# Token norms and router sums of a fused two-block transformer layer laid in four strips of 128 tokens

## The reference, cut to what matters

```python
def rms_norm(x, g):                       # five of these, over the 1024 channels of a token
    r = lax.rsqrt(jnp.mean(x * x, axis=-1, keepdims=True) + EPS)
    return x * r * g
# block 1
h = rms_norm(x, norm1_g); p = h @ w_in    # 1024 x 3328
...                                       # gMLP branch, S5 branch, gates, w_up_a, w_up_b, w_out
h2 = rms_norm(x, norm2_g)
probs = softmax(h2 @ w_router)            # 16 experts
gate, idx = lax.top_k(probs.T, 64)        # 64 tokens for each expert
...                                       # for each expert: silu(xs @ w_gate) * (xs @ w_up) @ w_down
x = rms_norm(x + scattered, final_g)
# block 2
u = rms_norm_2(x, norm1_gain); proj = u @ w_in_2
y_lru = rms_norm_2(scan(...) * gelu(g_lru), lru_norm_gain)    # over 512 channels
o = head_group_norm(retention(q, k, v), ret_norm_gain)        # 4 heads of 128 channels
x = x + concat(y_lru, o * silu(g_ret)) @ w_out_2
up = conv(rms_norm_2(x, norm2_gain) @ ffn_up_w)               # 1024 x 6144, two halves
x = x + (gelu(up_a) * up_v) @ ffn_down_w
return rms_norm_2(x, final_norm_gain)
```

## Time and profile before

| | |
|---|---|
| median of 3 runs | 1932.91 us (1932.58 to 1933.05) |
| profiled execution, its own time | 1933.91 us |
| span in its trace, first to last instruction | 1932.1 us |
| PE busy | 1750.1 us, 91% |
| DVE busy | 667.9 us, 35% |
| ACT busy | 443.6 us, 23% |
| DMA moved | 492.47 MB |
| mean granted clock of PE | 0.982 |

### The profile page before, as it was taken

How to read it: one execution, slowest core, us unless ns; L and a number is a source line. 1 busy time by engine, 2 the same in 40 slices (tenths; PEclk the granted TensorE clock), 3 DMA queues, 4 the chain that set the end, 5 groups by cost and what they waited for, 6 DMA issues and landing times. The chain is left out here.

```text
span 1932.1 us, 19429 instructions
## 1 busy us (share of the span) xinstructions
PE 1750.1 (91%) x8120; PEld 1045.2 (54%) x8120; DVE 667.9 (35%) x903; ACT 443.6 (23%) x546; POOL 0.2 (0%) x4
## 2 busy tenths in 40 slices
PE   5998997899998898988979889789999999999997
PEld 4877774434342332423324233247767778888885
DVE  6865463201011010100101001047735466555644
ACT  4433322101010000100001010055433343323332
POOL 0000000000000000000000000000000000000000
PEclk9999999899999999999999999999999999999999
DMA  4313644699999999999999999950412213232311
GB/s 160 99 48 107 218 136 184 261 428 428 427 428 429 429 428 429 428 429 428 428 428 429 428 428 428 428 220 28 153 44 88 87 66 109 87 109 87 109 44 44
DMA packets 76389, 492.47 MB, mean 255 GB/s; under 512 B 7472, under 2 KB 12592, under 8 KB 51504
## 3 DMA queue, kind: packets, MB, share of 16 engines
q1 hardware_dynamic: 76336, 491.71, 63.1%
HBM read 487.49 MB, written 2.10 MB: 253 GB/s over the span
## 5 line engine op out<-in xcount | busy, mean ns | idle before, releaser
L1166 PE MATMUL ps<-xs,xe 128*64 128x512 f32 x2048 | 462.9, 600 | 65.8 <-DMA xs<-w_up 33.2
L1166 PEld LDWEIGHTS ps<-xs,xe 128*64 128x64 f32 x2048 | 142.1, 137 | 379.2 <-issue 265.9
L1178 PE MATMUL ps<-xs,hidT 128*64 128x512 f32 x1024 | 229.7, 596 | 13.6 <-DMA xs<-w_down 8.9
L412 DVE TENSOR_TENSOR lo<-raw,hi 128x2048 fp32r<-128x2048 f32 (+1 forms) x73 | 164.9, 2259 | 217.7 <-ACT hi L403 210.6
L1394 DVE TENSOR_TENSOR hid<-hid,ps 128x512 f32<-128x512 f32 x32 | 20.6, 684 | 524.3 <-PE ps L1166 524.3
L403 ACT ACTIVATE hi<-raw 128x2048 fp32r<-128x2048 f32 (+1 forms) x73 | 137.9, 1889 | 232.0 <-PE ps L466 96.9
L466 PE MATMUL ps<-xh,hi 128*128 128x512 f32 x416 | 167.8, 403 | 10.3 <-DVE ga L921 5.8
L466 PE MATMUL ps<-xl,hi 128*128 128x512 f32 x416 | 164.3, 395 | 0.0
L442 PE MATMUL ps<-xh,hi 128*128 128x512 f32 x384 | 151.4, 394 | 4.3 <-ACT hi L403 3.2
L1178 PEld LDWEIGHTS ps<-xs,hidT 128*64 128x64 f32 x1024 | 74.0, 137 | 147.6 <-issue 127.7
L442 PE MATMUL ps<-xl,hi 128*128 128x512 f32 x384 | 150.2, 391 | 0.0
(11 more groups left out here) (415 smaller groups left out, 1783.6 us busy)
## 6 DMA issues: line engine op xcount, KB each, us to landing
xs<-w_up SPq DMA_DIRECT2D x64, 2048.0 KB, 32.8
xs<-w_gate SPq DMA_DIRECT2D x64, 2048.0 KB, 31.9
xs<-w_down SPq DMA_DIRECT2D x64, 2048.0 KB, 31.3
raw<-w_in SPq DMA_DIRECT2D x25, 1024.0 KB, 7.2
raw<-ffn_up_w SPq DMA_DIRECT2D x24, 1024.0 KB, 5.1
raw<-ffn_down_w SPq DMA_DIRECT2D x12, 1024.0 KB, 5.1
raw<-w_out SPq DMA_DIRECT2D x8, 1024.0 KB, 5.1
xin<-x_t SPq DMA_DIRECT2D x4, 512.0 KB, 7.4
```

The lines of the kernel that those rows point to most:

```text
L412: dve.tensor_tensor(lo[slot][:, 0:size], raw[:, raw_slot(n), 0:size], hi[slot][:, 0:size].bitcast(F32), ALU.subtract).then_inc(sem("lo_don ...
L1166: mm = pe.matmul(ps[64 * half:64 * half + 64, bank + b, :], xe[:, k, CAP * u:CAP * (u + 1)], xs[n % NXS][:, f:f + 512], start=(k == 0), st ...
L1178: mm = pe.matmul(ps[64 * nn:64 * nn + 64, YB, :], hidT[:, 4 * (c % 2) + kk, CAP * half:CAP * (half + 1)], xs[n % NXS][:, kk * D + nn * 512 ...
```

## The change

Sums go into four strips of 32 partitions, one for each 128 tokens, all in the same 128 columns of a bank. A strip's 32 rows are equal, so root and reciprocal need 128 columns in place of 512. Then four matmuls with a 32-row operand that has a one in its first row spread each strip back over all partitions, each into a bank of its own, and ACT copies the 512 values to SBUF.

```diff
@@ new helpers
+        def strip_sums(pe, i, bank):
+            for k in range(KD):
+                pe.wait_ge(sem("nrm_sq"), NSQ[i] + k + 1)
+                for t in range(NT):
+                    mm = pe.matmul(strip(bank, t), ones[:, 0:32], squares(i)[0][:, k, t * P:(t + 1) * P],
+                                   start=(k == 0), stop=(k == KD - 1))
+            mm.then_inc(sem("nrm_ps"), 1)
+        def strip(bank, t, c=0):
+            return ps[32 * t:32 * t + 32, bank, c:c + P]
+        def strip_spread(pe, r, bank, c):
+            for t in range(NT):
+                mm = pe.matmul(ps[:, bank + t, c:c + P], pick[32 * t:32 * t + 32], r[32 * t:32 * t + 32],
+                               start=True, stop=True)
+            return mm
+        def strip_root(act, i, bank):
...
+            act.activation(rs[0], ps[:, bank, 0:P], ACT.Sqrt, scale=1.0 / D, bias=eps).then_inc(sem("nrm_rms"), 1)
@@ norm 1, PE
-            norm_sums(pe, 0, QQ + 3)
+            strip_sums(pe, 0, QQ + 3)
+            def spread_first():
+                pe.wait_ge(sem("rb_done"), 1)
+                strip_spread(pe, rs[0], PP, SW)
+                pe.transpose(ps[:, PP, SW + P:SW + 2 * P], rs[0], ident).then_inc(sem("rt_ps"), 1)
             chunk_mms(pe, 1, QQ, 0, 4, xh, xl, True, closes=False,
-                      after={(0, 2): lambda: pe.wait_ge(sem("nrm_rms"), 1)})
-            pe.wait_ge(sem("rb_done"), 1)
-            for t in range(NT):
-                mm = pe.matmul(ps[:, PP, SW + t:SW + t + 1], rb[:, t * P:(t + 1) * P], ident[:, 0:1], start=True, stop=True)
+                      after={(0, 1): spread_first, (0, 2): lambda: pe.wait_ge(sem("nrm_rms"), 1)})
@@ router, PE
-                mm = pe.matmul(ps[o, LB, :], wrg[:, k, :], xt[:, k, :], start=(k < 4), stop=(k >= 4))
...
+                for t in range(NT):
+                    pe.matmul(strip(LB, t), wrg[:, k, :], xt[:, k, t * P:(t + 1) * P], start=(k == 0), stop=False)
+                pe.wait_ge(sem("nrm_sq"), KD + k + 1)
+                for t in range(NT):
+                    mm = pe.matmul(strip(LB, t), hot[:, 0:32], sqx[:, k, t * P:(t + 1) * P], start=False, stop=(k == KD - 1))
...
+            for bank in (SB, LB):
+                mm = pe.transpose(ps[:, bank, 0:P], part[:], ident)
@@ router, ACT
-            a(part[1][:], ps[:, SB, :], ACT.Copy).then_inc(sem("part_done"), 1)
@@ first norm of block 2, PE: after two tiles of chunk N2+1
+            def spread_two():
+                pe.wait_ge(sem("rms_step"), 1)
+                for q in range(4):
+                    pe.matmul(ps[:, QQ + q, 256:512], pick[32 * q:32 * q + 32], rr[32 * q:32 * q + 32], start=True, stop=True)
+                for b in range(2):
+                    mm = pe.transpose(ps[:, QQ + 1, b * P:(b + 1) * P], rr[:, b * P:(b + 1) * P], ident)
+                mm.then_inc(sem("rt_ps"), 1)
@@ LRU and heads, PE
-                    mm = pe.matmul(ps[:, 0, :], ones, xc[:, m, :], start=(m == 0), stop=(m == 3))
+                    for t in range(NT):
+                        mm = pe.matmul(strip(0, t), ones[:, 0:32], xc[:, m, t * P:(t + 1) * P], start=(m == 0), stop=(m == 3))
...
+                      after={(0, 0): head_vars, (0, 1): spread_lru, (0, 3): spread_heads})
-            pe.wait_ge(sem("mix_lo"), 4)
             pe.wait_ge(sem("yn_done"), RH)
-            chunk_mms(pe, N2 + 12, PP, 0, 4, mh, ml, closes=False)
+            chunk_mms(pe, N2 + 12, PP, 0, 4, mh, ml, closes=False, by_tile=("mix_lo", 1))
@@ FFN norm, PE
-            norm_sums(pe, 4, QQ + 3)
-            chunk_mms(pe, NFFN + 1, QQ, 0, 4, xh, xl, closes=False,
-                      after={(0, 2): lambda: pe.wait_ge(sem("nrm_rms"), 4)})
-            chunk_mms(pe, NFFN + 2, PP, 4, 4, xh, xl, opens=False, by_tile=("xl_done", 2 * KD + 5))
-            chunk_mms(pe, NFFN + 3, QQ, 4, 4, xh, xl, opens=False)
+            strip_sums(pe, 4, QQ + 3)
...
+            chunk_mms(pe, NFFN + 1, PP, 4, 4, xh, xl, opens=False, by_tile=("xl_done", 2 * KD + 5), after={1: spread_fourth})
+            pe.wait_ge(sem("spr_out"), 3)
+            for h in range(2):
+                chunk_mms(pe, NFFN + 2 + h, QQ, 4 * h, 4, xh, xl, opens=(h == 0), closes=(h == 1))
```

More of the change, by code:

```diff
@@ L265, in build @@
         sqx = at("sqx", [P, KD, SEQ], F32, B + 57)
-        part = [at(f"part{j}", [P, SEQ], F32, B + 51 + 2 * j) for j in range(2)]
+        part = at("part", [P, P], F32, B + 51)
         cst2 = at("cst2", [P, NCONST - NSMALL], F32, B + 38)
@@ L328, in build @@
         vmean = sm[:, 32:48]
+        hot = sm[:, 150:198]
         pick = sm[:, 256:384]
+        rs = [sm[:, 384 + 128 * j:512 + 128 * j] for j in range(2)]
         def lz(j):
@@ L477, in chunk_mms @@
                             mm = one(part, m, kk)
+                    if kk in after:
+                        after[kk]()
             elif each:
@@ L837, in first_dve @@
             dve.memset(eps, EPS).then_inc(sem("eps_done"), 1)
+            dve.memset(pick, 0.0)
+            L(dve.memset(hot, 0.0))
+            for h in range(4):
+                dve.memset(pick[32 * h:32 * h + 1], 1.0)
+            dve.memset(hot[:, 16:17], 1.0)
             dve.wait_ge(sem("cst_in"), 32)
@@ L1492, in head_vars, with spread_lru, spread_heads @@
                     pe.wait_ge(sem("csq_done"), h + 1)
-                    mm = pe.matmul(ps[32 * h:32 * h + 32, 1, :], ones[:, 0:32], kr[:, h, :], start=True, stop=True)
+                    for t in range(NT):
+                        mm = pe.matmul(strip(1, t, P), hot[:, 16 - h:48 - h], kr[:, h, t * P:(t + 1) * P],
+                                       start=(h == 0), stop=(h == RH - 1))
                 mm.then_inc(sem("hvar_ps"), 1)
-            def spread():
+            def spread_lru():
+                pe.wait_ge(sem("rb_done"), 2)
+                pe.wait_ge(sem("hstd_done"), 1)
+                strip_spread(pe, rs[0], 0, 2 * P).then_inc(sem("rt_ps"), 1)
+            def spread_heads():
                 pe.wait_ge(sem("rv_done"), 1)
-                pe.wait_ge(sem("lrms_done"), 1)
+                pe.wait_ge(sem("spr_out"), 2)
                 for h in range(RH):
-                    mm = pe.matmul(ps[:, h, :], pick[32 * h:32 * h + 32], rv[32 * h:32 * h + 32], start=True, stop=True)
+                    for t in range(NT):
+                        mm = pe.matmul(ps[:, t, h * P:(h + 1) * P], sel[32 * t:32 * t + 32, h, :], rs[1][32 * t:32 * t + 32],
+                                       start=True, stop=True)
                 mm.then_inc(sem("rv_ps"), 1)
@@ L1667, in second_act @@
                 a(xc[:, m, :], rA[:, m, :], ACT.Square).then_inc(sem("lsq_done"), 1)
+            make_hi(act, N2 + 12)
             take_o(3)
@@ L1702, in second_act @@
             new_tiles(range(4, KD))
-            make_hi(act, NFFN + 2)
-            norm_root(act, 4, QQ + 3)
+            strip_root(act, 4, QQ + 3)
+            act.wait_ge(sem("rt_ps"), 4)
+            a(r4[:].rearrange("p (t c) -> p t c", t=NT), ps[:, QQ:QQ + NT, P:2 * P], ACT.Copy).then_inc(sem("spr_out"), 1)
             def part(n, i, j, down=True):
                 p = j[0] % 2
-                if down:
-                    make_hi(act, n + 2, i)
-                else:
-                    make_hi(act, n + 3)
-                    make_hi(act, n + 4)
+                make_hi(act, n + 2, i)
                 act.wait_ge(sem("par_done"), lin(j, i, 1, 1))
@@ L1916, in second_dve @@
             new_rest(range(4, KD))
-            make_lo(dve, NFFN + 2)
-            dve.wait_ge(sem("nrm_rms"), 4)
-            L(dve.reciprocal(r4[:], r4[:]))
+            dve.wait_ge(sem("nrm_rms"), 3)
+            dve.reciprocal(rs[0], rs[0]).then_inc(sem("rb_done"), 1)
             for h in range(2):
@@ L1950, in part @@
                     last.then_inc(sem(("fa_done", "fv_done")[b]), 1)
[L1951 removed]
+                    if b == 0:
                         make_lo(dve, n + 4, i)
@@ L2009, in part @@
                     load_chunk(sp, n + 4 + h, i, ffn_down_chunk(w, lin(j, i, 512, -512), h))
-            for h in range(2):
-                for b in range(2):
-                    load_chunk(sp, NFFN + 2 * h + b, None, ffn_up_chunk(w, FF2 * b, h))
+            for b in range(2):
+                for h in range(2):
+                    load_chunk(sp, NFFN + 2 * b + h, None, ffn_up_chunk(w, FF2 * b, h))
             with sp.Fori(0, NJ // 2 - 1) as i:
```

132 lines of the change are left out of this document (55 added, 77 removed).

## The result

| | before | after |
|---|---|---|
| median | 1932.78 us, 4 runs (1932.58 to 1933.05) | 1902.47 us, 4 runs (1901.27 to 1903.23) |
| profiled execution | 1933.91 us, span 1932.1 | 1902.93 us, span 1901.2 |
| PE busy | 1750.1 us | 1724.2 us |
| mean granted clock | 0.982 | 0.986 |

The ratio is 0.984, 95% interval 0.9828 to 0.9853: 30.3 us less by the medians, beside 30.6 forecast.

What follows compares the result with a forecast made beforehand. Expert stage bound by 402 MB of weights, PE the bound before and after; 4.8 + 2.6 + 1.7 + 2.95 + 9.2 + 9.35 = 30.6 us less, median 1902.3 us, 8-in-10 range 1898 to 1912.

Steps and rivals of the forecast that it cites:

- Strips run four at once: Cost of strips on PE: four matmuls of 128 columns in four strips take 0.22 us together.
- Rivals C and D: C: only two of four strips overlap, 1916.3 us, chance 0.04. D: strips' passes run one after another, 1943.8 us, 0.03.
- The rule of the Trainium skill: Counter-rule: about 62 ns per matmul, so eight passes of four strips take 0.5 us and the gain is near 18 us.
- Norm 1: Block 1's first norm: sums in strips 4.8 us less, spreading matmuls and transpose even with the old turn.
- each us taken off PE in block 1: Block 1: PE is the bound, so each us taken off it is a us of the whole.
- block 2's norm: First norm of block 2: sums 3.4 us less, spread and transposes 0.45 us more, 2.95 us less in all.
- Router: Two terms: `logits(4)` and `(5)` inside chunk 20, 2.6 us less; the work behind chunk 20, 1.7 us less.
- Expert stage: Bound by its 402 MB of weights, fixed length of about 940 us, only moves along with the router's end.
- LRU and heads: Block 2, before chunk N2+12: 9.2 us less, 6.2 by an earlier start and 3.0 by the clock staying up.
- FFN: FFN norm and first chunks: sums 4.8 us less, spread 0.5 more, waits and low clock gone; 9.35 us less.
- A wait costs twice: Behind PE's wait for `ml` the granted clock is 0.50, costing 3.0 us more; 1.5 us behind the FFN wait.
- Rival A: Block 2's two chains are longer than summed, so waits and low clock partly stay: 7.5 us, 1909.8 us; chance 0.2.

Runs made afterwards that it cites:

- experiment 9: Kernel of experiment 8 plus zero-matrix matmuls in two block 1 waits and the last square on DVE, first filler one chunk early: 1900.48 us.
- experiment 4: Changed kernel with both copies of chunk N2+12 back in their old places, behind the roots and the reciprocals: 1901.22 us.
- experiment 2: Changed kernel with the FFN norm alone back at full width, new order of the first FFN chunks kept: 1904.64 us.
- experiment 1: Kernel before with only the changes of order (moved copies, wait by tile, new FFN chunk order), no strips: 1921.36 us, ratio 0.9942.
- experiment 7: Kernel before with five zero-matrix matmuls of 512 tokens in the wait for `ml` before chunk N2+12: 1930.14 us, ratio 0.9981.
- experiments 1 and 3: The second of these: changed kernel with LRU and head norms back at full width, moved copies and wait by tile kept: 1904.04 us.
- experiment 8: Changed kernel with the program's last norm in strips too, DVE multiplying from PSUM, run twice: 1896.94 us, again 1897.09 us.
- the second kernel of experiment 9: As the first kernel of experiment 9, but the five filling matmuls stand in chunk 6, where the wait is: 1897.28 us, ratio 0.9805.

## Why the prediction was right

The median was forecast at 1902.3 us and is 1902.5. That the two agree to 0.2 us is partly luck: four items that I had left at zero (-0.4, +1.6, -1.0, -0.4) nearly cancel, and the medians scatter by more than that. That the sum holds place by place, none of its six terms off by more than 0.6 us, is not luck.

- **Strips run four at once.** Forecast 0.22 us for four matmuls of 128 columns; in the router's first group one set follows the other by 0.219 us. Rivals C and D are out. The rule of the Trainium skill (page "TensorE: Matmul & The Clock Gate", section "Wait — 56ns, not 53.3ns?") that I had weighed against it gives about 62 ns for each matmul with hardware decode off; no run here shows which way that is set. Counted by instruction, which is two of the passes, the sets stand at 55 ns and those of the earlier trace rows at under 48. So even counted that way the rule did not bind here, the row was the right one to go by, and my reading of the rule by the pass made it look twice as bad as it is.
- **Norm 1** gave 0.6 us more than forecast: 4.6 us by the sums (4.8 forecast), 0.3 because this run came to them earlier, and some 0.5 because spread and transpose were cheaper than the turn, where I had them even. That all of it comes through has a condition that the prediction's "each us taken off PE in block 1" left out: the wait for `ga` (experiment 9) lets through only what the stores of SP, and DVE ahead of them, are earlier by. They were, from 129.21 to 123.80 us. At block 2's norm it is alike: 3.4 us by the sums as forecast, and the turn cost 0.1 us more in place of 0.45.
- **Router.** Both terms hold to 0.1 us. The first expert matmul came at 340.87 us, forecast 342.5: the low clock at the start of chunk 20 was absent, which I had only as a bound.
- **Expert stage.** Moved along as forecast. The rate is 428 GB/s in both, the length 918.1 us after 916.7, not the 940 us of the prediction, which divides all 402 MB by the rate although eight slots are filled before the stage starts. Only the change of length enters the sum.
- **LRU and heads.** The time is right (8.9 for 9.2), and the forecast start of chunk N2+12 is 1454.0 less the 13.1 us of lead at that point, 1440.9: measured 1440.98. The chain (reciprocals 0.95, copy 0.60, scalings 0.68 a tile) is as worked out, and so is the DVE's time to spare before PE's spread: 1448.7 to 1450.4 us in the working, 1.7 us, and 1.61 measured. Two sentences of the prediction forgot this spare time. Without cover, the copies would not put their 1.9 us into the chain but 0.2 (experiment 4: nothing), and a reciprocal of 3.37 us would make it 3.1 us late, not 4.8. Splitting the 8.9 by the runs: the order alone 6.7, of which the wait by tile is 1.6 where strips are in place; strips 2.2.
- **FFN.** 9.3 for 9.35: 4.1 by strips (4.8 - 0.5 forecast) and 5.2 by the order (3.2 + 1.5 + 0.35 forecast). What I had at nothing is the loop behind it: the gap at each of its turns grew from 0.31 to 0.38 us, and 0.4 us were given back in all. It goes with the strips of the FFN norm, since experiment 2 does not have it and experiment 1, order alone, does not either; why is open.
- **A wait costs twice** held for the wait of 4.45 us (experiment 7, 2.7 us of 3.0). It does not hold as a rule: see below.
- **Rival A** had 0.2 by narrow margins, 0.1 and 0.7 us. They were 0.3 us (first tile of `ml` at 1440.7, needed at 1440.98) and 0.5 us (high part at 1552.1, needed at 1552.6), small, but they held in every traced run that has both the strips and the wait by tile. Where PE does wait for a tile of `ml` (experiments 1 and 3) it starts 0.15 us behind it, so half of the 0.3 us is the hand-over itself.

## What to carry to other kernels

Before a reduction is made cheaper, separate what its width costs from what its place in the order costs: here 11 of 30 us came from order alone, and one of the moved pieces was worth nothing once the others were in. A quarter-width layout pays three times, in PE passes, in the root and in a reciprocal whose cost follows its columns, and costs one spread and one copy of about half a us each. It is free of waits where the result is needed later than that, and it paid even at the last norm, where the values are needed at once. A filled or shortened wait is a gain only up to the next wait whose end it does not move, and the engine named there need not be the cause: here the DVE stood behind SP's queue.

## What the runs showed of the hardware that was not expected

- **The low clock behind a wait is not certain.** The same wait of 3.13 us before chunk 20 has, in the windows just behind it, 0.57 in the kernel before, 1.00 in the changed kernel, and in two runs of one and the same kernel (experiment 8) 0.61 and 1.00:

```profile
294.80:298.90 4.10, 4.09 (x12) 3.15 (x12) 0.00 (x0) 0.00 (x0) 0.00 (x0) 0.61 0.75 260
```

```profile
295.40:298.40 3.00, 3.00 (x17) 2.24 (x21) 0.03 (x1) 0.00 (x0) 0.00 (x0) 1.00 0.73 218
```

  The wait of 2.7 us at the FFN had six slow passes behind it in the kernel before and none in experiment 7. Even a shorter wait can have the low clock: PE waits 1.84 us for `kr` in block 2 in every trace, and in two of the thirteen, the first run of experiment 8 and the second kernel of experiment 9, the clock is 0.50 behind it, which costs 1.6 us. The windows of the first run of 8:

```profile
1388.00:1391.40 3.40, 3.40 (x9) 2.02 (x7) 1.97 (x1) 0.00 (x0) 0.00 (x0) 0.50 0.13 11
```

  Ahead of chunk matmuls, waits of 1.3 us (every trace) and 1.45 us (one) had no slow passes, unfilled ones of 4.4 to 8.3 us always 5 to 13. So about 1 to 3 us (5 to 13 passes at 0.43 in place of 0.23 us) belong to each long wait, and how many, changes with the run. The Trainium skill (page "TensorE: Matmul & The Clock Gate", section "What's actually happening") says that one and the same kernel shows different numbers of slow matmuls in different runs; the traces agree, and add that behind the waits of 1.84, 2.7 and 3.1 us it may be none at all.
- **The scatter has an address.** From the first matmul of block 2's first chunk to one in the last chunk (2448 chunk matmuls on) the changed kernel took 597.7 us, experiment 4 597.6 and the second run of 8, which differs only behind that point, 597.7. The first run of 8, the same kernel, took 599.3 us, by the low clock just shown. The expert stage, with the same code, took 916.5 to 919.0 us in the eleven new traces and the two old ones, and in the kernels with strips at norm 1 the start of chunk 1 lay between 34.5 and 36.5 us. So a difference of 1 us in block 2 can be read from one trace only at its own place and with the granted clock beside it; over the whole of block 2, or in the median of five runs, it can't.
- **A reciprocal follows its width** to a few hundredths of a us: 0.18 us at 4 columns, 0.95 at 128, 3.35 at 512.
